# The four RWKV up projections ahead of the attention ones, and p turned before the output projection, in a three-layer fused block

## The reference

```python
z = rmsnorm_2(h, mix_pre_norm) @ w_in
o_attn = dilated_attention_branch(z_attn)          # 256 wide: 4 heads of 64
o_rwkv = rwkv7_time_mix(z_rwkv, ...)               # 512 wide
gate_attn, gate_rwkv = jnp.split(jax.nn.sigmoid(z_gate), 2, axis=-1)
merged = gate_attn * (o_attn @ w_attn_up) + gate_rwkv * (o_rwkv @ w_rwkv_up)
h = h + rmsnorm_2(merged @ w_out, mix_post_norm)
f = rmsnorm_2(h, ffn_pre_norm)
f = jnp.square(jax.nn.relu(f @ w_ff_in)) @ w_ff_out
h = h + rmsnorm_2(f, ffn_post_norm)
e = (p @ w_ple) * jax.nn.sigmoid(h @ w_ple_gate)
h = h + rmsnorm_2(e, ple_post_norm)
```

## Time and profile before

| | |
|---|---|
| median of 3 runs | 932.37 us (931.05 to 932.65) |
| the profiled execution: its own time | 933.87 us |
| the profiled execution: span of the trace | 932.1 us |
| TensorE busy | 911.1 us, 98% of the span |
| VectorE busy | 654.1 us, 70% |
| ScalarE busy | 510.7 us, 55% |
| granted TensorE clock, mean | 0.999 |

### The profile page before, as it was taken

One profiled execution on the slowest core, in us unless ns is written; L12 is line 12 of the kernel. 1 busy time (PEld: TensorE's weight loads), 2 busy tenths in 40 slices (PEclk: granted clock), 3 DMA queues, 4 the chain that ended last, 5 costly groups with the idle time before them and its releaser, 6 DMA issues.

```text
span 932.1 us, 19580 instructions
## 1 busy us (share of the span) xinstructions
PE 911.1 (98%) x8673; PEld 888.5 (95%) x8673; DVE 654.1 (70%) x772; ACT 510.7 (55%) x608; POOL 2.1 (0%) x14
## 2 busy tenths in 40 slices
PE   8899999999999999999999999999999999999997
PEld 7899999999999999999998999899899999999997
DVE  2897987775677667767789876557777665465565
ACT  3535445444554567954485764376756553455445
POOL 0000000000000000000000000000000000000000
PEclk9999999999999999999999999999999999999999
DMA  9999646875568644367634453234444556556421
GB/s 338 356 361 357 199 136 226 280 224 167 165 202 261 196 137 136 123 200 230 192 124 142 138 172 96 88 95 139 145 156 139 181 186 223 180 182 218 165 92 46
DMA packets 153439, 172.30 MB, mean 185 GB/s; under 512 B 4000, under 2 KB 137692, under 8 KB 153228
## 3 DMA queue, kind: packets, MB, share of 16 engines
q1 hardware_dynamic: 151696, 167.43, 55.8%
q10 hardware_dynamic: 1660, 3.63, 1.1%
HBM read 170.00 MB, written 1.05 MB: 184 GB/s over the span
## 4 chain that ended last, share of the span: by engine, by line
PE 76%; DVE 12%; ACT 6%; issue 4%; DMA 1%; ACTq 1%; DVEq 0%; POOL 0%; POOLq 0%
PE pj L2749 62%; DVE w_lo L1530 3%; ACT w_hi L1024 2%; DMA work<-in_x_dram 1%; PE pj L2703 1%; PE pj L2704 1%; PE pj L2705 1%; ACTq L987 1%; PE m_all L2439 1%; PE m_all L2422 1%; PE m_all L2169 1%; DVE work L1977 1%; PE pj L2532 1%; DVE small L1978 1%; ACT work L1310 0%
## 5 line engine op out<-in xcount | busy, mean ns | idle before, releaser
L1530 DVE TENSOR_TENSOR w_lo<-raw,w_hi 128x2048 fp32r<-128x2048 f32 (+1 forms) x126 | 285.1, 2268 | 126.8 <-ACT w_hi L1024 126.3
L2749 PE MATMUL pj<-h_hi,w_hi 128*128 128x256 f32 x1160 | 329.0, 284 | 2.5 <-issue 1.5
L2749 PE MATMUL pj<-h_lo,w_hi 128*128 128x256 f32 x1160 | 323.9, 279 | 0.0
L2749 PE MATMUL pj<-h_hi,w_lo 128*128 128x256 f32 x1160 | 323.6, 279 | 0.0
L1024 ACT ACTIVATE w_hi<-raw 128x2048 fp32r<-128x2048 f32 (+1 forms) x126 | 237.8, 1890 | 51.8 <-PE pj L2749 23.4
L2749 PEld LDWEIGHTS pj<-h_hi,w_hi 128*128 128x128 f32 x1160 | 217.3, 187 | 5.8 <-issue 3.6
L2749 PEld LDWEIGHTS pj<-h_lo,w_hi 128*128 128x128 f32 x1160 | 217.4, 187 | 0.3
L2749 PEld LDWEIGHTS pj<-h_hi,w_lo 128*128 128x128 f32 x1160 | 217.3, 187 | 0.2
L2749 PE MATMUL pj<-y_lo,w_hi 128*128 128x256 f32 x624 | 174.6, 280 | 0.0
L2749 PE MATMUL pj<-y_hi,w_hi 128*128 128x256 f32 x592 | 165.9, 280 | 1.1 <-issue 1.1
L2749 PE MATMUL pj<-y_hi,w_lo 128*128 128x256 f32 x592 | 165.2, 279 | 0.0
(11 more groups left out here) (427 smaller groups left out, 1148.3 us busy)
## 6 DMA issues: line engine op xcount, KB each, us to landing
raw<-in_odd_in_w_dram SPq DMA_DIRECT2D x28, 1024.0 KB, 5.3
raw<-in_w_in_dram SPq DMA_DIRECT2D x23, 1024.0 KB, 5.4
raw<-in_ada_w_dram SPq DMA_DIRECT2D x22, 1024.0 KB, 7.5
raw<-in_w_ff_in_dram SPq DMA_DIRECT2D x16, 1024.0 KB, 5.4
raw<-in_w_ff_out_dram SPq DMA_DIRECT2D x16, 1024.0 KB, 5.2
raw<-in_even_in_w_dram SPq DMA_DIRECT2D x13, 1024.0 KB, 6.2
raw<-in_even_out_w_dram SPq DMA_DIRECT2D x8, 1024.0 KB, 5.8
raw<-in_odd_out_w_dram SPq DMA_DIRECT2D x8, 1024.0 KB, 5.5
```

Source lines behind the costliest of these rows:

```text
L1530: V.tensor_tensor(lo[:, 0:n], raw_of(u)[:, 0:n], hi[:, 0:n].bitcast(F32), ALU.subtract).then_inc(done, 1)
L2749: m = nc.tensor.matmul(to, a_, b_, start=(s == 0 and q == 0 and (fb == 0 or not together)), stop=(s == len(steps_) - 1 and q == 2), skip_g ...
```

## The change

The fourth RWKV up projection, which stood between the second and the third attention job, is created and run after `at_t` 3 and ahead of `at_o` 3. `au_first` 0 moves ahead of `at_t` 3, `au_first` 1 behind `at_o` 3. The mark `late` and the split entries of `ru` 2 go, so that its job entry splits; the entry `split("hi", "au", 3)` moves behind the last `au` job. `turn_p` moves from behind wo1 to the front of wo0.

```diff
     up_rw(1)
     up_rw(2)
-    late("ru", 2)
-    split("hi", "ru", 2)
-    split("lo", "ru", 2)
+    step("au_first", 0)
     step("at_t", 3)
-    for i in range(2):
-        step("au_first", i)
+    up_rw(3)
     step("at_o", 3)
+    step("au_first", 1)
     step("au_first", 2)
     step("mixed", 3)
     up_at(0)
     up_at(1)
-    up_rw(3)
-    split("hi", "au", 3)
     up_at(2)
     step("au_first", 3)
     up_at(3)
+    split("hi", "au", 3)
     split("lo", "au", 3)
...
     for i in range(4):
+        if i == 0:
+            step("turn_p")
         job("wo", "out", i, "F", [unit(ins["w_out_2"][0], 0, KD, i * CB, CB)], KD, 16, lambda xc: ("merged_lo", (xc - 16) // 2 + 1))
-        if i == 1:
-            step("turn_p")
```

## The result

| | before | changed |
|---|---|---|
| median of 20 runs | 931.95 us (931.0 to 933.09) | 934.01 us (932.69 to 935.33) |
| ratio | | 1.0019, 95% interval 1.0013 to 1.0025 |
| span of the profiled execution | 932.1 us | 933.3 us |

The changed kernel is 0.19% slower, 1.8 us by the ratio (1.2 to 2.3; the medians differ by 2.06). The interval excludes no change, so a small loss is clear of the scatter.

What follows compares the result with a forecast made beforehand. TensorE, busy 98% of the span, was taken to bound the kernel. wo1 1.96 us late less 0.43 for p's turn gave 1.5 us later on a median of 932.37: 933.9 us, range 932.0 to 936.3 (8 in 10), 70% chance.

Steps and rivals of the forecast that it cites:

- The three waits: TensorE before both halves of `at_t` 3 and before `at_o` 3: 1.1 us, about 0.2 left, 0.9 won if nothing else binds.
- The merge starts later: DVE's first line of the merge of `au` jobs starts at 679.55 against 677.92.
- Waits within wo0: TensorE waits some 0.2 us for wo0's first low part and 1.15 at its fifth chunk; wo0 ends at 689.93.
- wo1's weights: ACT makes their high part behind the fourth merged job; wo1 starts at 691.2 against 689.24, 1.96 us late.
- p's turn: Four transposes moved from behind wo1 to before wo0, hidden in TensorE's wait there; gives back 0.43 us.
- The normalisation: Its first line, behind wo3, starts at 711.1 against 709.62; nothing after it gives the 1.5 us back.
- The loads (rival c): Feed-forward weight loads become a second bound; +3.5 us in all, 935.9, if they take 10.5 us to land; 11%.
- The clock (d): Rival: TensorE's clock falls in the new waits of 1.2 and 1.3 us; 936 us or more; 3%.
- (a): Rival: stalls removed decide, merge and wo1's weights not late; TensorE wins 0.9 us, 931.5; 6%.
- (b): Rival: the merge is late but wo1's weights are hidden; +0.3 us, 932.7; 10%.
- the slack: Time to spare before the change: 0.4 us for the merge at wo0's fifth chunk, 0.4 or so for wo1's weights.
- The prediction's reckoning with a faster rate: At 109 ns per 256-column matmul instead of 120, the merge starts 0.4 us earlier and the cost is 1.1 us.

Runs made afterwards that it cites:

- the third experiment: The changed kernel with the mark `late` and the two split entries of `ru` 2 put back; 933.34 us, ratio 1.0014.
- the kernel with the job order alone: The kernel before with only the change's order of up jobs and without the three `ru` 2 entries; 932.61 us, ratio 1.0013.
- the first experiment: The changed kernel with the high part of wo1's weights back between the second and third merged job; 933.34 us, ratio 1.001.
- the sixth: The kernel before with only `au_first` 0 moved ahead of the last transposes, `at_t` 3; 931.93 us, ratio 0.9996.
- the second experiment: The kernel before with the high part of wo1's weights moved behind the fourth merged job; 933.29 us, ratio 1.0015.
- the second execution: The kernel before, unedited, run and profiled again; 931.72 us.
- the version with the transposes in the gap: The kernel before with p's four transposes on TensorE moved ahead of `at_t` 3; 931.67 us, ratio 0.9995, and 931.32 us, ratio 1.0, in a second set.

## Why the prediction was right, and where it was off

The median came out at 934.01 us against 933.9, inside the range, and as no change by the 0.2% bound (ratio 1.0019). The mechanism came as forecast: the late merge, then the late weights of wo1. That the two numbers agree to 0.1 us is luck, as told below. Step by step, with positions counted from the low part of wo0 (674.34 before, 673.92 after):

- The three waits: 0.2 us was to be left of them, 0.17 is. Right.
- The merge starts later: forecast 5.21 us behind the ruler's start (679.55), measured 5.20 (679.12). The added neighbours on DVE cost nothing, as said, and the third experiment agrees.
- Waits within wo0: forecast 0.2 and 1.15, measured 0.29 and 0.89.
- wo1's weights: forecast 16.86 (691.2), measured 16.90 (690.82), with a wait of 1.15 instead of 1.3. The first two experiments show that this term hangs on one entry: 1.33 us when it is taken back in the changed kernel (1.18 without the slower pace of its trace, 36.76 - 35.58), and 1.17 (36.17 - 35.00) when it is made in the old one, where 0.95 was expected.
- p's turn: forecast to give back 0.43. Taking it back costs 0.29 in the changed kernel, 0.44 at equal pace; between the kernel with the job order alone and the first experiment, which differ in nothing else, it is 36.01 - 35.58 = 0.43. wo2 had no wait. On the table load the trace of the changed kernel says what that of before said: the copy behind it starts 1.29 us after its start, and a drain of another 1.38 (the Trainium skill, "ScalarE: Activation LUTs", What ACT_TABLE_LOAD costs) doesn't show. Had it come, it would have been just hidden: the low part of wo2's weights ends at 695.09 (692.80 + 2.29), and wo2 starts at 696.55.
- The normalisation: forecast at 36.76, measured 36.91, of which 0.16 is the slower pace behind wo1.
- One sum is not in line with its terms: `au_first` 2 starts at 677.75 by them, and 677.85 was taken for wo0. Nothing hangs on it, because TensorE waits for the first low part either way.
- The loads (rival c) came nearer but did not bind: ACT waits 1.77 us for the first feed-forward unit, and DVE still idles 3.09 us before the normalisation. The clock (d) stayed at 1.00, its upper level, through the new waits. (a) and (b) are answered by the sixth and by the second experiment.

Off was the reference, not the changed kernel. The sum took before's stretch as 35.28 us, and the second execution has 35.00; against that the change costs 1.91 instead of 1.5, or 1.76 with the third experiment's 36.76 in place of 36.91. It splits into three parts that the experiments measure one by one: the order of the jobs +1.01 (36.01), p's turn -0.43 (35.58), wo1's high part +1.18 (36.76), and 0.15 for the pace of the changed kernel's execution (36.91). By the ratio of the times it is 1.8.

The mis-sized term is the slack. I counted some 0.4 us at the fifth chunk and at wo1's weights by 0.120 us a matmul; at 0.117 it is 0.16 and nothing. Of a late chain every bit beyond the slack is paid, so a slack that is overstated by 0.3 understates the cost by as much. What hid the error is that I set the 1.5 on a median of 932.37 from three runs, and 20 runs gave 931.95: a base 0.42 too high and a cost 0.3 to 0.4 too low, which cancelled.

The prediction's reckoning with a faster rate had the sign wrong. By 109 ns a matmul it put the cost at 1.1, less than at 120; the rate was 117, and the cost was higher than 1.5. It made only the changed kernel's way to the merge shorter. But TensorE paces the kernel before all the way to wo1, so a faster rate shortens that one too, while the changed kernel waits for DVE and ACT from the merge to wo1, and their times stay.

Not tried: a shorter merge on DVE (for instance low parts written by another engine). No order tried here wins the last 0.7 us of TensorE's waits in front of the transposes and the value products without a loss behind them.

## What to carry to other kernels

Before work is moved into an engine's wait, find the next chain that starts behind it and its slack: 2.9 us of matmuls put into a wait of 0.3 us pushed back a merge whose slack was 0.2 to 0.4 us. Where the queues are in program order, an entry that splits weights for the next job is part of the move: put behind the last step of a late chain, it became the end of that chain. Small independent work, such as four transposes, fits a short wait that long work doesn't; here that is shown by the traces and is too small for the times. And a slack of a few tenths read from one execution is no more certain than that execution's pace: read it from two.

## What the runs showed of the hardware that was not expected

The same matmuls of 256 columns start every 120 ns in one execution and every 117 ns in another of the same program at a granted clock of 1.00 in both: 683.48 to 689.24 for the 48 of wo0, against 681.03 to 686.71 in the second, which has 0.08 us of wait in it. The slow rate held in the first profile from 677 to 695 us, where p's transposes stand. That is 0.3 us over the stretch, a sixth of what was to be told apart.

There is a rate between the two as well, about 118 ns: in the changed kernel from wo0 to the end of wo3, in both executions of the version with the transposes in the gap from wo1 on, in most others within wo0 or wo1 only. Between two executions with the same instructions there, 20.01 and 19.85 us from wo1 to the normalisation, it makes 0.16 us. So one profiled execution is a ruler with an error of 0.2 to 0.3 us. The cause stays open.
